# Second block of a two-block network: branch scales moved onto the attention's output, and norm rows turned by products with a diagonal matrix

## The reference

```python
x = first_block(...)                    # ends with x = rmsnorm(x, norm_final)
h = modulate(rms_norm(x, norm1_g), shift1, scale1)      # h * (1 + scale) + shift
qa, ka, va, qb, kb, vb = split(h @ w_in)
o_a = windowed_gqa(qa, ka, va, sink_a, t5_table)        # 8 heads of 64
o_b = neighbourhood_attention(qb, kb, vb, rpb_b)        # 8 heads of 64
mixed = concatenate([rms_norm(o_a, out_norm_a), rms_norm(o_b, out_norm_b)], axis=-1)
x = x + gate1 * (mixed @ w_out)
h2 = modulate(rms_norm(x, norm2_g), shift2, scale2)
x = x + gate2 * peer(h2, w_query, sub_keys, u_experts, v_experts)

def rms_norm(x, g):
    return x * lax.rsqrt(jnp.mean(x * x, axis=-1, keepdims=True) + EPS) * g
```

## Time and profile before

| | us |
| --- | --- |
| median of 3 runs | 1759.57 |
| lowest and highest | 1758.71, 1759.61 |
| the profiled execution | 1759.11 |
| its span | 1757.8 |
| PE busy in it | 1726.8 |
| DVE busy in it | 1346.3 |
| ACT busy in it | 917.9 |

### The profile page before, as it was taken

How to read it: one execution, slowest core, us unless ns; L and a number is a source line. 1 busy time by engine, 2 the same in 40 slices (tenths; PEclk the granted TensorE clock), 3 DMA queues, 4 the chain that set the end, 5 groups by cost and what they waited for, 6 DMA issues and landing times.

```text
span 1757.8 us, 33401 instructions
## 1 busy us (share of the span) xinstructions
PE 1726.8 (98%) x11704; PEld 1585.4 (90%) x11704; DVE 1346.3 (77%) x2383; ACT 917.9 (52%) x1612; POOL 65.4 (4%) x116
## 2 busy tenths in 40 slices
PE   9999999999999999999989999999999999999997
PEld 7899899989999899989879999999999988888886
DVE  7975788878976788878684999988888866666666
ACT  4345444444454444455553555567777654445553
POOL 1000001000000122100000000000000000000000
PEclk9999999999999999999999999999999999999999
DMA  6655588755445599844334455553433355555554
GB/s 217 209 188 196 170 311 274 258 180 168 156 156 168 205 306 318 268 150 156 121 129 159 156 179 181 184 173 133 144 133 132 133 193 194 194 193 191 191 193 153
DMA packets 90940, 330.24 MB, mean 188 GB/s; under 512 B 11097, under 2 KB 11273, under 8 KB 90402
## 3 DMA queue, kind: packets, MB, share of 16 engines
q1 hardware_dynamic: 79346, 287.49, 48.3%
q0 software_dynamic: 10240, 36.26, 6.3%
q10 hardware_dynamic: 1264, 5.24, 0.8%
HBM read 326.81 MB, written 6.09 MB: 189 GB/s over the span
## 4 chain that ended last, share of the span: by engine, by line
PE 81%; DVE 14%; ACT 2%; issue 2%; DVEq 0%; ACTq 0%
PE bank L207 24%; PE bank L208 24%; PE bank L209 24%; DVE Z L86 6%; DVE w_lo L184 4%; PE bank L1712 3%; PE bank L276 1%; ACT w_hi L179 1%; DVE yc L86 1%; PE bank L483 1%; PE bank L1297 1%; DVE x L86 1%; PE bank L781 1%; PE bank L268 1%; DVE rows L86 0%
## 5 line engine op out<-in xcount | busy, mean ns | idle before, releaser
L184 DVE TENSOR_TENSOR w_lo<-raw,w_hi 128x1024 fp32r<-128x1024 f32 x546 | 661.5, 1221 | 160.2 <-ACT w_hi L179 159.3
L179 ACT ACTIVATE w_hi<-raw 128x1024 fp32r<-128x1024 f32 x546 | 573.8, 1052 | 257.9 <-PE bank L209 183.9
L207 PE MATMUL bank<-u_hi,w_hi 128*128 128x256 f32 x2416 | 698.0, 289 | 6.2 <-ACT Z L86 1.4
L209 PE MATMUL bank<-u_hi,w_lo 128*128 128x256 f32 x2416 | 684.1, 283 | 0.0
L208 PE MATMUL bank<-u_lo,w_hi 128*128 128x256 f32 x2416 | 683.8, 283 | 0.0
L207 PEld LDWEIGHTS bank<-u_hi,w_hi 128*128 128x128 f32 x2416 | 463.5, 192 | 18.7 <-issue 8.9
L208 PEld LDWEIGHTS bank<-u_lo,w_hi 128*128 128x128 f32 x2416 | 463.5, 192 | 4.8 <-issue 2.4
L209 PEld LDWEIGHTS bank<-u_hi,w_lo 128*128 128x128 f32 x2416 | 463.1, 192 | 0.0
L207 PE MATMUL bank<-w_hi,a_hi 128*128 128x512 f32 x744 | 290.5, 390 | 0.7 <-DVE u_lo L1798 0.7
L208 PE MATMUL bank<-w_lo,a_hi 128*128 128x512 f32 x744 | 290.1, 390 | 0.0
L209 PE MATMUL bank<-w_hi,a_lo 128*128 128x512 f32 x744 | 289.4, 389 | 0.0
(11 more groups left out here) (285 smaller groups left out, 1728.8 us busy)
## 6 DMA issues: line engine op xcount, KB each, us to landing
raw<-stream SPq DMA_DIRECT2D x546, 512.0 KB, 3.3
gate<-w_ada POOLq DMA_DIRECT2D x48, 512.0 KB, 6.5
t_rows<-t_by_distance POOLq DMA_DIRECT2D x8, 256.0 KB, 4.0
rpb_rows<-rpb_pad POOLq DMA_DIRECT2D x8, 224.0 KB, 3.9
gains<-gains POOLq DMA_DIRECT2D x3, 512.0 KB, 5.2
bias_b<-rpb_rows POOLq DMA_DIRECT2D x16, 96.0 KB, 7.4
bias_a<-t_rows POOLq DMA_DIRECT2D x1, 1536.0 KB, 13.7
x<-x_in ACTq DMA_DIRECT2D x2, 512.0 KB, 4.4
```

Source lines behind the costliest of these rows:

```text
L179: nc.scalar.activation(w_hi[:, s, :], raw[:, s, :], ACT.Copy).then_inc(s_hi, 1)
L184: nc.vector.tensor_tensor(w_lo[:, s, :], raw[:, s, :], w_hi[:, s, :].bitcast(F32), ALU.subtract).then_inc(s_split, 1)
L207: M.matmul(o, lh, rh, start=start, stop=False, skip_group_check=True)
L209: return M.matmul(o, ll, rh, start=False, stop=stop, skip_group_check=True)
```

## The change

It has five parts.

1. *Turning by a diagonal.* xn (and later x) is no longer scaled ahead of the transposes. VectorE multiplies the identity by the 128 factors of a tile (`diagonal`), and `turn_scaled` makes products src x diagonal, which turn and scale at once: eight products of 128 columns a tile in place of eight transposes. Tile 0 is turned as soon as its root is there, tile 1 after 14 fillers (28 and 24 fillers before).
2. *Roots tile by tile.* `both_roots` works on one column. The root of tile 0 stands behind the third sum, that of tile 1 behind the split of `splits[0]`. All squares go to ScalarE. `split_lo(splits[1])` moves ahead of `modulated_to_u`.
3. *Branch scales on og.* The factor of a branch goes into the product that makes og. So the square of o and `branch_scales` come before og, and a unit has one step more.
4. *One accumulation.* Branch A's first three pieces are accumulated, then, behind the whole attention of branch B, the fourth, and the four pieces of branch B are added in the same banks 0 to 3. `add_out` (gate, then sum) replaces `add_branch`, four times instead of eight.
5. *Banks.* The second norm is turned into banks 6, 7, 2, 3; the third query piece and the fourth go to bank 6.

```diff
+        diag = space[:, 3, 0:NT * P].rearrange("p (t n) -> p t n", t=NT)
+
+        def diagonal(tt, r):
+            return VE.go((r, (s_kept, 16)), V.tensor_scalar, diag[:, tt, :], ident, st[:, 3, tt:tt + 1], None, ALU.mult)
+
+        def turn_scaled(src, tt, banks, *marks):
+
+            PE.wait(*marks)
+            done = []
+            for g, b in enumerate(banks):
+                if tt == 0:
+                    take(b)
+                for e in range(2):
+                    k = 2 * g + e
+                    i = M.matmul(bank[b][:, e * T + tt * P:e * T + (tt + 1) * P], src[:, tt, k * P:(k + 1) * P],
+                                 diag[:, tt, :], start=True, stop=True, skip_group_check=True)
+                done.append(PE.done(i))
+            return done
...
+        def both_roots(tt, squared):
+
+            c = slice(tt, tt + 1)
+            m1 = VE.go((squared,), V.tensor_tensor, st[:, 0, c], st[:, 5, c], st[:, 6, c], ALU.add)
+            m = VE.go((squared,), V.tensor_tensor, st[:, 9, c], st[:, 7, c], st[:, 8, c], ALU.add)
+            m1 = VE.go((m1,), V.tensor_scalar, st2[:, 1, c], st[:, 0, c], 1.0 / D, EPS, ALU.mult, ALU.add)
+            m = VE.go((m,), V.tensor_scalar, st[:, 4, c], st[:, 9, c], 1.0 / D, None, ALU.mult)
+            m = VE.go((m, m1), V.scalar_tensor_tensor, st[:, 1, c], st2[:, 1, c], EPS, st[:, 4, c],
+                      ALU.mult, ALU.add)
+            return diagonal(tt, root(st[:, :, c], 1, m)), m1
...
+                    if tt and n:
+                        split_hi(first_split)
+                    squared = junk_mark[0]
                     sum_of(tt, n)
+                    if tt and not n:
+                        diags[0], _ = both_roots(0, squared)
                     square_of(x, 5, x_marks, tt, n)
-                    if tt + n < NT:
-                        square_of(xn, 7, g_marks, tt, n)
+                    square_of(xn, 7, g_marks, tt, n)
...
+        first_split = at["piece"] + AHEAD + 1
         splits = held_pieces(*last_downs, sums())
+        assert splits[0] == first_split and len(splits) == 2
+        turn_banks = (6, 7, 0, 1)
+        turn_scaled(xn, 0, turn_banks, diags[0], *g_marks[0])
         take(5)
-        keep_clock(5, 28)
...
+        keep_clock(5, 14)
+        split_hi(splits[1])
         split_lo(splits[0])
-        h_ready = modulated_to_u(xn, (m, m1), scaled, 0)
+        diags[1], mean_mark = both_roots(1, junk_mark[0])
+        turned = turn_scaled(xn, 1, turn_banks, diags[1], *g_marks[1])
         split_lo(splits[1])
+        h_ready = modulated_to_u(turned, turn_banks, scaled, 0)
...
+            got["squares", kind, tt] = AC.go((m,), S.activation, junk[:, tt, :], o, ACT.Square,
+                                             accum_out=sst[:, kind, 0, tt:tt + 1])
+            yield
             cols = slice(kind * W, (kind + 1) * W)
-            og_m = VE.go((m, own.get("og_free")), V.tensor_tensor, og[:, tt, :], o, gains_b[:, 1, cols], ALU.mult)
+            og_m = VE.go((m, got["r", kind, tt], own.get("og_free")), V.scalar_tensor_tensor, og[:, tt, :], o,
+                         sst[:, kind, 3, tt:tt + 1], gains_b[:, 1, cols], ALU.mult, ALU.mult)
             yield
...
-                  10: (a1, a0), 11: (a1, a0), 12: (a1, b0), 13: (a0, a1), 14: (a1, b0), 15: (b1, b0),
+                  10: (a1, a0), 11: (a1, a0), 12: (a1, b0), 13: (a0, a1), 14: (a0, a1, b0), 15: (b1, b0),
...
+            if n == 13:
+                branch_scales(0, slice(0, NT))
...
+        acc = acc_banks()
+        for tt in range(NT):
+            PE.wait(*got["mixed", 0, tt])
+        for k, side in enumerate(((b0,), (b1,), (b0, b1, b0))):
+            out_piece(k)
             for u in side:
-                next(u, None)
-        next(b1, None)
-        next(b0, None)
-        add_branch(0, r_a, 0, 0), add_branch(0, r_a, 0, 1)
+                next(u)
+        next(b1)
+        branch_scales(1, slice(0, 1))
+        next(b0)
+        next(b1)
+        run(b0)
+        branch_scales(1, slice(1, 2))
+        next(b1)
+        out_piece(KW - 1)
         split(at["piece"] + AHEAD)
...
         def branch_sums():
-            add_branch(0, r_a, 1, 0), add_branch(0, r_a, 1, 1)
-            r_b[0] = branch_scales(1, slice(0, 1))
-            yield
+            add_out(0, 0)
             run(b1)
+            square_of(x, 5, x_marks, 0, 0)
+            yield
+            add_out(0, 1)
+            square_of(x, 5, x_marks, 0, 1)
             PE.wait(*got["mixed", 1, 1])
-            take(0), take(1)
-            add_branch(1, r_b[0], 0, 0), add_branch(1, r_b[0], 0, 1)
-            squares(x, space_lo[0], 5, x_marks, 0)
-            yield
-            r_b[1] = branch_scales(1, slice(1, 2))
-            add_branch(1, r_b[1], 1, 0)
-            yield
-            add_branch(1, r_b[1], 1, 1)
+            yield
+            add_out(1, 0)
+            diags[0] = diagonal(0, token_roots(junk_mark[0], slice(0, 1)))
+            square_of(x, 5, x_marks, 1, 0)
+            split_hi(q_splits[0]), split_hi(q_splits[1])
+            yield
+            add_out(1, 1)
+            square_of(x, 5, x_marks, 1, 1)
             yield
...
+                             acc, branch_sums(), ahead=False)
+        assert splits == q_splits
+        turn_banks = (6, 7, 2, 3)
+        turn_scaled(x, 0, turn_banks, diags[0], *x_marks[0])
+        take(5)
+        keep_clock(5, 14)
         split_lo(splits[0])
...
+        diags[1] = diagonal(1, m)
+        turned = turn_scaled(x, 1, turn_banks, diags[1], *x_marks[1])
         split_lo(splits[1])
-        h2_ready = modulated_to_u(xn, (m, m1), scaled, 1)
+        h2_ready = modulated_to_u(turned, turn_banks, scaled, 1)
         split_lo(splits[2])
...
-            b = 4 + (f // 2) % 2
+            b = 4 + (f // 2) % 2 if f > 2 else 6
```

More of the change, by code:

```diff
@@ L1153, in lower_tile @@
                                         u_hi[:, k, :].bitcast(F32), ALU.subtract)))
-            for g in range(KD // 2):
-                b = (6, 7, 0, 1)[g]
-                i = transposes(b, [src[:, tt, k * P:(k + 1) * P] for k in (2 * g, 2 * g + 1) for tt in range(NT)],
-                               marks)
+            for g, b in enumerate(banks):
+                i = turned[g]
                 for e in range(2):
@@ L1400, in branch_scales, with out_piece, add_out @@
                       ALU.mult, ALU.add)
-            return root(sst[:, kind, :, tiles], len(marks), m)
-        def out_pieces(kind):
-            acc = acc_banks()
-            for tt in range(NT):
-                PE.wait(*got["mixed", kind, tt])
-            for k in range(kind * KW, (kind + 1) * KW):
-                piece_a(acc, (mx_hi, mx_lo), (k,), D, k % KW == 0, k % KW == KW - 1)
-                yield
-        def add_branch(kind, r, tt, n):
+            m = root(sst[:, kind, :, tiles], len(marks), m)
+            for tt in range(NT)[tiles]:
+                got["r", kind, tt] = m
+        def out_piece(k):
+            piece_a(acc, (mx_hi, mx_lo), (k,), D, k == 0, False)
+        def add_out(tt, n):
             cols = slice(n * 512, (n + 1) * 512)
-            b = (2 * tt + n, (4, 6, 0, 1)[2 * tt + n])[kind]
-            m = VE.go((bank_marks[tt][n], r, ada_rest, got.get(("hT", n))), V.scalar_tensor_tensor,
-                      added[:, n, :], bank[b][:, :], sst[:, kind, 3, tt:tt + 1], gate1[:, cols],
-                      ALU.mult, ALU.mult)
+            b = 2 * tt + n
+            m = VE.go((bank_marks[tt][n], ada_rest, got.get(("hT", n))), V.tensor_tensor, added[:, n, :], bank[b][:, :],
+                      gate1[:, cols], ALU.mult)
             free[b] = (m,)
@@ L1451, in build @@
+        next(b1)
[6 more added lines that the diff above has]
+        out_piece(KW - 1)
         split(at["piece"] + AHEAD)
-        next(b1, None)
-        r_b = [None, None]
         scaled = column_scale(1, ada_rest)
+        q_splits = [at["piece"] + AHEAD + 1 + j for j in range(3)]
         def branch_sums():
-            add_branch(0, r_a, 1, 0), add_branch(0, r_a, 1, 1)
-            r_b[0] = branch_scales(1, slice(0, 1))
+            add_out(0, 0)
+            run(b1)
+            square_of(x, 5, x_marks, 0, 0)
```

45 lines of the change are left out of this document (10 added, 35 removed).

## The result

| | before | changed |
| --- | --- | --- |
| median, us | 1759.64 (12 runs) | 1763.45 (12 runs) |
| lowest, highest | 1758.71, 1762.39 | 1763.06, 1765.25 |
| profiled execution, its span | 1759.11, 1757.8 | 1763.09, 1761.8 |
| mean granted clock in it | 0.999 | 0.996 |

The ratio is 1.0021, with a 95% interval of 1.0013 to 1.0029: slower by 3.8 us. The forecast was 1763.5. The runs of the changed kernel form two groups, seven from 1763.06 to 1763.59 and five from 1764.71 to 1765.25. The mean granted clock of the seven is 0.996 to 0.998, of the five 0.995 to 0.996.

A forecast was written before the change was run, and what follows sets the result against it. TensorE, busy 98% of the span, was taken to bound the kernel, so only its short idle stretches move: 1.9 - 0.1 + 3.5 - 1.3 = 4.0 us on 1759.11, median 0.46 higher, forecast 1763.5, range 1760.5 to 1766.

The forecast's parts named there:

- handover, with what is given back: Start of the second block: first hT 1.9 us later through VectorE's chain, less 0.1 us given back.
- turning of og: Branch A, before the scores: new TensorE waits of 0.9 us for bank 5 and 1.2 us for mx_lo, plus 2.1.
- branch B and outputs: Up to the last output product: old waits go (-3.0), og delay (+2.1), late output splits (+2.4), fewer form changes (-0.2).
- tail: Last output product to the second norm's first hT: the longer chain itself adds 0.1 us.
- bank 6: Third query piece starts at 914.05 in place of 915.32, no longer behind bank 5's eviction: minus 1.3 us.
- the second split, no longer owed behind hT: Handover: w_lo split now ahead of hT; TensorE lost 0.1 us for it before, which is given back.
- the forecast's 851.65: Branch A: time mx_lo has been read and bank 0 is free for the scores, where TensorE would be at 850.5.
- The second head product: Branch B: waits 1.3 us, to 881.8, because ScalarE squares o before copying the bank this product reads.
- The waits for w_lo: First output accumulation: TensorE waits 1.9 and 0.5 us for the last two pieces' splits, plus 2.4.
- First rival, VectorE's amount of work: Branch B and outputs: the 5.8 us taken off VectorE comes off the path, median 1756.4; chance 0.17.
- Second rival, the clock: Handover and tail: idle TensorE drops the clock to 1.2 GHz, up to 4.6 us more, 1765.5 to 1768; chance 0.08.
- Third rival, slow true products: Tile turns of 3.55 us: about 1.3 us more at the handover, 2.0 in the tail, median 1766.8; chance 0.03.

The follow-up runs named there:

- a_covered: Changed kernel, order untouched, with fillers in four idle places (9 before turning tile 0, 3 and 5 before branch B's head products, 7 before the late output piece): 1762.24 us.
- b_bank6: Kernel before with one edit, third and fourth query piece in bank 6: 1758.04 us, ratio 0.9991.
- a_og_banks: Changed kernel with branch A's og turned in banks 6 and 7 in place of 0 and 2: 1762.94 us, ratio 1.0019.
- a_fillers: Changed kernel with three fillers ahead of branch B's first head product and five ahead of the second: 1763.64 us, ratio 1.0025.
- b_new_handover: Kernel before with only the changed kernel's handover (roots tile by tile, turning by diagonal, 14 fillers, moved splits): 1762.38 us, ratio 1.0015.
- a_all: Changed kernel with old handover, branch A's og in its own banks, an earlier output split, and 3 and 5 fillers ahead of branch B's head products: 1758.36 us.
- a_oh_og_early: Changed kernel with old handover, branch A's og turned in its own two banks, and an earlier output split, without added branch B fillers: 1761.82 us.

## Why the prediction was right, and where it was not

The median came out at 1763.45 for a forecast of 1763.5. Step by step, the "clean" column is counted in a_covered, where the clock does not fall (but for its last term):

| term | forecast | clean |
| --- | --- | --- |
| handover, with what is given back | +1.8 | +1.0 |
| turning of og | +2.1 | +2.0 |
| branch B and outputs (-3.0 + 2.1 + 2.4 - 0.2) | +1.3 | +1.3 |
| tail | +0.1 | -0.2 |
| bank 6 | -1.3 | -1.3 (b_bank6) |
| falls of the clock, in the profiled execution | 0 | +1.4 |
| sum | 4.0 | 4.2 |

- *Handover, a mis-sized term.* The mechanism is right: the root of tile 0 between the sums moves the fourth sum. It came 1.9 us later and not 2.1, because the root and the diagonal take 2.5 us (776.40 to 778.92) and not 2.65, and VectorE was free a little sooner. From the fourth sum to hT it takes 6.2 us, not 6.5. So hT is 1.34 us later and not 1.9. And the second split, no longer owed behind hT, gives 0.36 back (+ 10.14 less + 8.81 is 1.33; at vaT it is 0.97), where I took 0.1. In the kernel before that time is lost at the product of 792.08, which starts right behind the first of three splits in a row (790.81 plus 1.22).
- *Turning of og.* 0.75 us marked for bank 5 and 1.07 for mx_lo, against 0.9 and 1.2. a_og_banks shows the second cause by taking it away. By its own terms the forecast's 851.65 should be 851.54 (850.85 plus 0.69), so the wait 1.0, nearer to the 1.07.
- *Branch B.* The second head product was forecast for 881.8 in the clock of before, which is + 104.8, or + 105.8 with the measured 1.0 of the handover; it starts at + 105.76. The waits for w_lo are marked 1.76 and 0.17; counted from the end of the last issue, as the forecast counts, they are 1.9 and 0.3, forecast 1.9 and 0.5. They were not to be seen in the changed kernel's own profile; it took executions in which the clock stayed up till there (a_og_banks, a_fillers) to see them.
- *Tail and bank 6.* Small, and as said within 0.3.
- *First rival, VectorE's amount of work.* False: 3.6 us less of it on VectorE, and waits for the same engine.
- *Second rival, the clock.* I gave it 0.08, for two places, since TensorE had idled 2.04 us at a clock of 1.00 in the earlier trace rows. That was one execution. The idle 2.05 us of the new handover is followed by a fall in two profiles (b_new_handover, a_og_banks) and by none in three. The wait of about 2.03 us for mx_lo in the order of before is followed by one in two of four. Its price, up to 4.6, was too high: 1.2 us at the handover. And the place that cost most, the two head products of branch B with waits of 0.75 and 1.14 us ahead of them, was not on my list: a fall in four of the five profiles without fillers there (not in a_og_banks). That is the step which failed: I took an idle time as harmless because one row showed it so, and looked only at the long ones. That the waits are part of the cause is shown: with fillers in them (a_fillers, a_all, a_covered) the same head products ran at 1.00 in all three profiles.
- *Third rival, slow true products.* False: 1.8 us a tile. The Trainium skill (TensorE: Matmul & The Clock Gate, Terms) has "4× faster for FP32" for the transpose mode; here it is 0.225 against 0.111 us, twice, so the trace does not agree.

The sum of 4.2 less the 0.4 us by which the second block started sooner is 3.8; the spans differ by 4.0, and the rest lies behind the queries. So the number was right in part by luck: 1.2 us too much for the sum of the parts (4.0 for 2.8), and 1.4 us for the clock left out. The range from 1760.5 has no working either; the forecast's own bounds give 1759.9. What happened in the five runs above 1764.7 stays open: no profile of one of them exists. Their mean clock, 0.995 to 0.996, is a little lower than that of the other seven, as a second fall would make it; a late start of the second block (0.4 to 1.6 us) would fit the time too.

## What to carry to other kernels

Taking work off an engine that is busy 13.1 of 14.0 us brings nothing when what TensorE waits for is the last item in that engine's order; read the order and ask what stands last. When a change opens a stretch in which TensorE has nothing to do, fill it with products that compute nothing, even where it is only 1 or 2 us long, and compare kernels with all such places filled: eight fillers were worth over 3 us of median here, nearly as much as the whole change. Filling only one of the places may do no more than move the fall to the next (a_fillers). And count from a common point in both traces, not from zero.

## What the runs showed of the hardware that was not expected

The clock fell to 1.2 GHz behind idle stretches as short as 1.76 us (a_fillers, between 894 and 895; not behind the same 1.76 us in a_og_banks) and behind two waits of 0.75 and 1.14 us with products of 64 columns and transposes between (the changed kernel, between 884 and 885), and stayed there for 3 to 7 us while TensorE was busy throughout. The same stretch in the same code brings it down in one execution and not in the next. The Trainium skill (TensorE: Matmul & The Clock Gate, Part 1) says of the gate's window that "it's free-running", so that the same program can meet it at another point; no run here shows the window, but the traces are in keeping with it, as the same 2.05 us of idle time ends with a fall in two profiles of five. What a fall costs depends on what lies beside it: 1.2 us at the handover, 1.4 in branch B of the changed kernel, 1.5 behind the wait for mx_lo, 2.6 in a_oh_og_early, where less waiting was left to hide it.
